# Thirty-two experts of a two-block kernel: a fifth pair of weight buffers, four of them rotating, and the first item's rows gathered ahead

## What is computed

```python
# t: the 256 tokens after norm and modulation; w_g, w_u: 32 x 1024 x 256, w_d: 32 x 256 x 1024
p_group = softmax(tf @ w_rg + b_rg)              # one of 4 groups
pv, pi  = top_k(softmax(le_g), 2)                # two of the 8 experts of that group
combine = sum(one_hot(ids, 32) * wts[..., None], axis=1)
for e in range(32):
    he  = silu(t @ w_g[e]) * (t @ w_u[e])
    out = out + combine[:, e:e + 1] * (he @ w_d[e])
```

## Time and profile before

| what | value |
|---|---|
| median of the timed runs | 1992.12 us (1991.62 to 1996.06, 3 runs) |
| the profiled execution's own time | 1992.81 us |
| its span, first to last instruction | 1990.9 us |
| PE busy | 1849.2 us, 93% of the span |
| chain that ended last | PE 86%, issue 4%, DVE 4%, DMA 2% |
| DMA | 345.07 MB, mean 173 GB/s over the span |
| PE on L1192, L1177, L1217 in the chain | 5%, 3%, 2% |
| stretch from first pick to the last item's products | about 565 to 843 us |

### The profile page before, as it was taken

The page is one execution under the profiler, slowest core; times in us unless marked ns, Lnnn a source line. Parts: engine busy times, 40 slices in busy tenths (PEclk is TensorE's granted clock), DMA queues, the critical chain, the costliest instruction groups (busy, mean ns, idle before and its releaser), DMA issues.

```text
span 1990.9 us, 33082 instructions
## 1 busy us (share of the span) xinstructions
PE 1849.2 (93%) x12610; PEld 1348.9 (68%) x12610; DVE 1035.5 (52%) x2332; ACT 551.4 (28%) x1185; POOL 54.2 (3%) x76
## 2 busy tenths in 40 slices
PE   6999999999987788899999899999999999999998
PEld 4878788757755566554564688887444465788886
DVE  3366573387442223444778877775987326333311
ACT  3343400172130111221570333332000226244310
POOL 0000000000000000000000011111000000000000
PEclk8999999999998899999999999999999999999999
DMA  9444483423459999630204122223764030144441
GB/s 372 177 190 195 185 359 149 169 86 157 197 241 425 421 418 390 258 127 0 85 2 190 64 84 85 84 84 138 306 252 170 2 108 1 50 155 155 165 187 48
DMA packets 38531, 345.07 MB, mean 173 GB/s; under 512 B 4231, under 2 KB 9102, under 8 KB 10382
## 3 DMA queue, kind: packets, MB, share of 16 engines
q1 hardware_dynamic: 37550, 334.02, 42.7%
q10 hardware_dynamic: 864, 9.44, 1.1%
HBM read 380.14 MB, written 1.05 MB: 191 GB/s over the span
## 4 chain that ended last, share of the span: by engine, by line
PE 86%; issue 4%; DVE 4%; DMA 2%; PEld 2%; ACT 1%; DVEq 0%; SPq 0%; PEldq 0%; ACTq 0%
PE bank L672 49%; PE bank L1428 13%; PE bank L1192 5%; PE bank L1177 3%; PE bank L1217 2%; PE bank L793 2%; PEld bank L672 2%; PE bank L1393 1%; PE bank L1302 1%; PE bank L1310 1%; DMA ring<-in_ada 1%; PE bank L1153 1%; PE bank L1400 1%; PE bank L898 1%; DVE ring L2135 1%
## 5 line engine op out<-in xcount | busy, mean ns | idle before, releaser
L672 PE MATMUL bank<-hn,ring 128*128 128x256 f32 (+2 forms) x2080 | 514.3, 407 | 9.8 <-ACT hn L1526 4.6
L672 PE MATMUL bank<-arena,ring 128*128 128x256 f32 (+2 forms) x1600 | 467.3, 449 | 17.8 <-issue 13.9
L672 PEld LDWEIGHTS bank<-hn,ring 128*128 128x128 f32 (+1 forms) x2080 | 395.3, 191 | 119.2 <-issue 68.6
L672 PEld LDWEIGHTS bank<-arena,ring 128*128 128x128 f32 (+1 forms) x1600 | 298.0, 188 | 180.4 <-issue 148.2
L1428 PE MATMUL bank<-ring 128*128 128x256 f32 x704 | 160.7, 381 | 1.2 <-DVE ring L2762 0.6
L1428 PEld LDWEIGHTS bank<-ring 128*128 128x128 f32 x704 | 133.7, 191 | 21.6 <-issue 2.1
L2022 DVE SCALAR_TENSOR_TENSOR bank<-ring,c_rows 128x1024 f32<-128x1024 f32 x96 | 118.1, 1231 | 21.5 <-DMA ring<-in_ada 16.7
L1428 PE MATMUL bank<-hn,ring 128*128 128x256 f32 x528 | 123.0, 383 | 3.8 <-ACT hn L1882 3.8
L2022 DVE SCALAR_TENSOR_TENSOR ring<-ring,c_rows 128x1024 f32<-128x1024 f32 x96 | 117.2, 1221 | 0.0
L1506 ACT ACTIVATE hn<-resid 128x256 f32<-128x256 f32 (+1 forms) x48 | 22.6, 485 | 336.5 <-DVE resid L2113 336.5
L1428 PEld LDWEIGHTS bank<-hn,ring 128*128 128x128 f32 x528 | 101.4, 192 | 18.5 <-issue 4.6
(11 more groups left out here) (434 smaller groups left out, 2072.5 us busy)
## 6 DMA issues: line engine op xcount, KB each, us to landing
ring<-in_ada SPq DMA_DIRECT2D x28, 2048.0 KB, 8.2
ring<-in_up SPq DMA_DIRECT2D x44, 1024.0 KB, 4.8
ring<-in_egu SPq DMA_DIRECT2D x20, 2048.0 KB, 16.3
ring<-in_edn SPq DMA_DIRECT2D x32, 1024.0 KB, 14.2
hn<-in_egu ACTq DMA_DIRECT2D x15, 2048.0 KB
arena<-in_egu SPq DMA_DIRECT2D x11, 2048.0 KB, 13.9
ring<-in_down SPq DMA_DIRECT2D x16, 1408.0 KB, 9.3
ring<-in_adat SPq DMA_DIRECT2D x8, 2048.0 KB, 11.8
```

What stands on the lines that cost most here:

```text
L672: last = mm(out, lhs(i), rhs(i), start=i == 0, stop=i == k - 1)
```

## The change

- A fifth pair of buffers. `gu_more` is a new gate_up buffer in `arena`, which grows by 3328 columns (13 KB per partition); the new down buffer is the upper half of the ring's slot 5. The space comes from the scratch that is set aside for descriptors: `dynamic_dma_scratch_size` goes from its default of 16384 bytes per partition to 1024. A sum buffer of the norm (`sq_acc`) moves to the end of `arena`.
- Items 0 to 4 take a pair each, item e from 5 on takes pair `(e - 5) % 4`, over items take pair 4, whose gate_up buffer is the one over `hn`.
- The order becomes 0 to 4, 5, 6 o0, 7 8 o1, 9 10 o2, 11 12 o3, and so on, with two over items after 20, 24 and 28 and none after 30.
- SP loads gate_up 0, down 0, gate_up 1, gate_up 2, down 1 to 4 and gate_up 3 ahead of `iota`, gate_up 4 into `hn` after it.
- PE waits for both halves of `pick`, gathers the 32 rows of item 0 into bank 6 (16 small matmuls), then block k = 0 of the gather of all, then `step(0)`, then blocks 1 to 7. ACT copies the first rows to `x_t[0]` and does item 0's Silu between blocks 2 and 3.
- Four semaphores that nothing used are gone.

```diff
+OVER_BUFFER = 4
+
+
 def item_order():
 
-    first, pairs = 4, (NE - 4) // 2
-    order, over = list(range(first)), NE
-    for pair in range(pairs):
-        order += [first + 2 * pair, first + 2 * pair + 1]
-        for _ in range(pair < pairs - 1) if pair not in (4, 9) else range(2):
+    order, over = list(range(OVER_BUFFER + 1)), NE
+    for item in range(OVER_BUFFER + 1, NE):
+        order.append(item)
+        for _ in range(0 if item % 2 or item > NE - 4 else 2 if item in (20, 24, 28) else 1):
             order.append(over)
             over += 1
     assert over == ITEMS and len(order) == ITEMS
@@ -65,7 +67,7 @@
 
 
 ORDER = item_order()
-BUFFER = [item if item < 4 else 3 if item >= NE else (item - 4) % 3 for item in ORDER]
+BUFFER = [item if item < 5 else OVER_BUFFER if item >= NE else (item - 5) % OVER_BUFFER for item in ORDER]
 USE = [BUFFER[:i + 1].count(b) for i, b in enumerate(BUFFER)]
 BEFORE = [max((j for j in range(i) if BUFFER[j] == b), default=None) for i, b in enumerate(BUFFER)]
 AT = {item: i for i, item in enumerate(ORDER)}
...
 SLOTW = 4096
+MORE = 3328
...
-        arena = sb("arena", [P, 12288])
+        arena = sb("arena", [P, 12288 + MORE])
...
+            if q == 0:
+                return ring[:, 6 * SLOTW - SLOTW // 2:]
+            q -= 1
             return ring[:, 2 * SLOTW + q * SLOTW // 2:2 * SLOTW + (q + 1) * SLOTW // 2]
...
-        sq_acc = out_tmp.rearrange("p a t -> p (a t)")
+        sq_acc = arena[:, 12288 + MORE - 2 * T:]
...
+        gu_more = arena[:, 12288 + MORE - 2 * T - SLOTW:12288 + MORE - 2 * T]
...
-            return (gu_arena, slot(1), slot(0), hn[:, :, :].rearrange("p k t -> p (k t)"))[q]
+            return (gu_more, gu_arena, slot(1), slot(0), hn[:, :, :].rearrange("p k t -> p (k t)"))[q]
...
             sp.wait_ge(phase, 3 * (MOE_PHASE - 2))
             load_gate_up(0)
+            load_down(0)
+            load_gate_up(1)
             sp.wait_ge(slot_free[1], used[1] + 1)
-            load_gate_up(1)
+            load_gate_up(2)
             sp.wait_ge(slot_free[2], used[2] + 1)
-            for i in range(2):
-                load_down(i)
+            for e in (1, 2):
+                load_down(e)
             sp.wait_ge(slot_free[3], used[3] + 1)
-            for i in range(2, 4):
-                load_down(i)
+            for e in (3, 4):
+                load_down(e)
             sp.wait_ge(slot_free[0], used[0] + 1)
-            load_gate_up(2)
+            load_gate_up(3)
             sp.wait_ge(phase, 3 * (MOE_PHASE - 1))
             sp.dma_start(iota, dr["iota"]).then_inc(s["moe_iota"], 16)
             sp.wait_ge(s["tok_mm"], 1)
-            load_gate_up(3)
-
-            for e in range(4, NE + 1):
+            load_gate_up(4)
+
+            for e in range(5, NE + 1):
                 if e < NE:
                     sp.wait_ge(s["moe_h"], BEFORE[AT[e]] + 1)
                     load_gate_up(e)
-                if e >= 5:
+                if e >= 6:
                     sp.wait_ge(s["moe_y"], BEFORE[AT[e - 1]] + 1)
                     load_down(e - 1)
...
-                    if i >= 1:
+                    if i == 0:
+                        pe.wait_ge(s["moe_Xev"], 1)
+                    else:
                         pe.wait_ge(s["moe_xt"], i)
...
-                            last = mm(bank[x][CAP * q:CAP * q + CAP, 0:P], x_t[x][:, k, :] if i else xs[:, k, 0:CAP],
+                            last = mm(bank[x][CAP * q:CAP * q + CAP, 0:P], x_t[x][:, k, :],
...
-            step(0)
+            pe.wait_ge(s["tok_ev"], 1)
+            pe.wait_ge(s["moe_G"], TT)
+            for k in range(KD):
+                for t in range(TT):
+                    last = mm(bank[6][:, k * CAP:(k + 1) * CAP], h_tok[:, t, k * P:(k + 1) * P], pick[:, t, 0:CAP],
+                              start=t == 0, stop=t == TT - 1)
+            last.then_inc(s["moe_X"], 1)
+            for k in range(KD):
+                if k >= 4:
+                    pe.wait_ge(s["moe_Xev"], k - 2)
+                if k == 1:
+                    step(0)
+                for t in range(TT):
+                    last = mm(bank[2 + k % 4][:, :], h_tok[:, t, k * P:(k + 1) * P], pick[:, t, :], start=t == 0, stop=t == TT - 1)
+                last.then_inc(s["moe_X"], 1)
+                if k == 4:
+                    pe.wait_ge(s["route_dve"], 4)
+                    mm(bank[7][0:NE, NE + 2:NE + 3], C("trix", NE)[:, 0:NE], cnt[0:NE, 1:2], start=True, stop=True) \
+                        .then_inc(s["route_pe"], 1)
+
...
             pe.wait_ge(s["route_dve"], 5)
             token_rows()
+            pe.wait_ge(s["moe_Xev"], KD + 1)
             mm(bank[5][:, 0:4 * OVER], ones[0:NE, :], table[0:NE, :], start=True, stop=True).then_inc(s["route_pe"], 1)
...
+            act_e.wait_ge(s["moe_X"], 1)
+            fn(x_t[0], bank[6][:, 0:KD * CAP].rearrange("p (k x) -> p k x", k=KD), ACT.Copy).then_inc(s["moe_Xev"], 1)
             for k in range(KD):
                 if k == 1:
                     act_e.wait_ge(s["route_dve"], 3)
                     fn(g4b, g4a, ACT.Exp)
                     fn(t2d, t2d, ACT.Exp).then_inc(s["route_act"], 1)
-                act_e.wait_ge(s["moe_X"], k + 1)
+                if k == 3:
+                    act_e.wait_ge(s["moe_h"], 1)
+                    fn(hsil[:, 0, :], bank[0][:, 0:64], ACT.Silu).then_inc(s["moe_silu"], 1)
+                act_e.wait_ge(s["moe_X"], k + 2)
                 fn(xs[:, k, 0:NPOS], bank[2 + k % 4][:, :], ACT.Copy).then_inc(s["moe_Xev"], 1)
...
+                    if i > 0:
+                        fn(hsil[:, i % 2, :], bank[i % 2][:, 0:64], ACT.Silu).then_inc(s["moe_silu"], 1)
...
-                        over_load(next_over[i], w_gate_up(3), "egu", gu_landed[3])
+                        over_load(next_over[i], w_gate_up(OVER_BUFFER), "egu", gu_landed[OVER_BUFFER])
...
-                        over_load(next_over[v], w_down(3), "edn", dn_landed[3])
+                        over_load(next_over[v], w_down(OVER_BUFFER), "edn", dn_landed[OVER_BUFFER])
...
-            pool.wait_ge(s["moe_Xev"], KD)
+            pool.wait_ge(s["moe_Xev"], KD + 1)
...
-    nc = bacc.Bacc("TRN2", target_bir_lowering=False, num_devices=1)
+    nc = bacc.Bacc("TRN2", target_bir_lowering=False, num_devices=1, dynamic_dma_scratch_size=1024)
```

More of the change, by code:

```diff
@@ L286, in build @@
         gqa_landed = [sem(f"gqa{i}_landed") for i in range(KVG)]
-        gu_landed = [sem(f"gate_up{i}_landed") for i in range(4)]
-        dn_landed = [sem(f"down{i}_landed") for i in range(4)]
+        gu_landed = [sem(f"gate_up{i}_landed") for i in range(OVER_BUFFER + 1)]
+        dn_landed = [sem(f"down{i}_landed") for i in range(OVER_BUFFER + 1)]
         phase = sem("phase_ended")
         names = """
-            vec_turned vec_ready csil_zeroed csil_ready rows_ready ada_mm ada_rows ada_cols ada_ready
+            vec_turned csil_zeroed csil_ready rows_ready ada_mm ada_rows ada_cols ada_ready
             sq_ready ss_ready std_ready hn_scaled hn_ready rope_reduced rope_sin
-            dt_pe dt_dve dt_act group_done gsm_ready
+            dt_pe dt_dve dt_act gsm_ready
             ssm_z ssm_zs ssm_x ssm_acc ssm_taps ssm_skip ssm_conv ssm_tok ssm_bcb ssm_xw ssm_E ssm_Ex ssm_from ssm_state ssm_stT ssm_seg
-            ssm_exp ssm_M ssm_yd ssm_yoff ssm_yo ssm_y ssm_sq ssm_ss ssm_std ssm_normed
+            ssm_exp ssm_M ssm_yd ssm_yoff ssm_y ssm_sq ssm_ss ssm_std ssm_normed
             out_mm out_sig out_ev gemm_mm gemm_ev
@@ L1144, in _ @@
             mm(bank[7][0:NE, NE + 1:NE + 2], sel_both, ones[:, 0:1], start=True, stop=True).then_inc(s["route_pe"], 1)
-            pe.wait_ge(s["tok_ev"], 1)
-            for k in range(KD):
-                if k >= 4:
-                    pe.wait_ge(s["moe_Xev"], k - 3)
-                for t in range(TT):
-                    if k == 0:
-                        pe.wait_ge(s["moe_G"], t + 1)
-                    last = mm(bank[2 + k % 4][:, :], h_tok[:, t, k * P:(k + 1) * P], pick[:, t, :], start=t == 0, stop=t == TT - 1)
-                last.then_inc(s["moe_X"], 1)
-                if k == 4:
-                    pe.wait_ge(s["route_dve"], 4)
-                    mm(bank[7][0:NE, NE + 2:NE + 3], C("trix", NE)[:, 0:NE], cnt[0:NE, 1:2], start=True, stop=True) \
-                        .then_inc(s["route_pe"], 1)
-            pe.wait_ge(s["moe_Xev"], KD)
-            def token_rows():
-                for b, pair in ((6, (pos_a, pos_b)), (7, (t2b, t2c))):
-                    for x, value in enumerate(pair):
-                        for t in range(TT):
-                            last = mm(bank[b][:, x * T + t * P:x * T + (t + 1) * P], value[:, t, 0:1].to_broadcast([P, P]), ident,
-                                      start=True, stop=True)
-                last.then_inc(s["moe_rows"], 1)
             def combine(v):
@@ L1219, in step, with token_rows @@
                     last.then_inc(s["moe_y"], 1)
-            step(0)
```

(13 more changed lines are left out.)

11 lines of the change are left out of this document (6 added, 5 removed).

## The result

| | before | after |
|---|---|---|
| median of 5 runs each | 1996.06 us (1991.62 to 1996.96) | 2005.96 us (2002.77 to 2007.68) |
| ratio of the runs | 1 | 1.0046, 95% interval 1.0033 to 1.0059 |
| span of the profiled execution | 1990.9 us | 2004.2 us |

The change costs 9.2 us (6.6 to 11.8). I had forecast 1.4 us, which can't be told from no change, and a range up to 2001.0: the measured change is well clear of no change, and 2005.96 lies outside the range. Part of the miss in absolute time is the base: before's three runs had a median of 1992.12, five have 1996.06. The rest is the forecast.

What follows compares the result with a forecast made beforehand. It took weight delivery by DMA to bound places 1 to 17 and PE pauses, inferred as late instructions, places 20 to 46. +2.9 at place 20 and -1.5 after gave +1.4 us: 1993.5 us, range 1984 to 2001.

Steps and rivals of the forecast that it cites:

- `iota`: SP's queue ahead of the gather: one pair more lands `iota` at 569.6, `pick` 4.8 us later, PE begins at 572.6.
- Rival 1: SP's queue: `iota` lands beside the other loads, `pick` is not late, everything to place 1 4.8 us earlier; 1988.7, chance 0.07.
- The gather of the first rows: PE ahead of place 1: small gather 6.6 us with 5 us at half clock; place 1 at 597.6, +9.7.
- rival 3: Gather: instruction pauses in blocks 1 to 7, perhaps half clock throughout the small gather and block 0; slower, 2000.5, chance 0.31.
- The buffer freed early: After early `step(0)`: gate_up buffer free about 2.8 us earlier than 585.73, at 582.9; DMA idle again until place 1 is multiplied.
- To the last place: Places 1 to 20: weights still decide, place 20 at 698.9 against 695.96, so +2.9 from +9.7 at place 1.
- line of delivery: Places behind the three pairs loaded over items: DMA's delivered weights set PE's pace, coming 1.6 us later for the same item.
- rival 2: Places 1 to 20: 16.1 us of weight waits and their half clock fall away, place 20 about 690; 1984.5, chance 0.23.
- Places 20 to 46: Last 26 places: fourth rotating pair fills DMA holes, transfers end some 10 us earlier; -1.5 us, between -4 and +3.
- the four numbers: Predicted whole times: forecast 1993.5, rival 1 1988.7, rival 2 1984.5, rival 3 2000.5 us.

Runs made afterwards that it cites:

- e1: After without the gather of the first rows: fifth pair, its item order and its loads, with before's gather and step(0); ratio to before 0.9998, -0.4 us.
- e5: Before with `iota` late, by a dummy pair of loads (3.1 MB, read by nobody) ahead of it on SP's queue; ratio to before 1.0022, +4.4 us.
- e4: After plus eight matmuls with unread results while PE waits for `pick`, to keep the clock up; ratio to before 1.0029, +5.8 us.
- e2: Before with only the gather of the first rows and step(0) moved ahead, four pairs and old order kept; ratio to before 1.0035, +7.0 us.
- e3: After with `iota` in a buffer of its own, loaded some 70 us earlier; ratio to before 1.0017, +3.4 us.
- e9: Before with SP's weight loads from item 4 on cut to a sixteenth of their columns, result not the kernel's; ratio to before 0.9677, -64.5 us.
- e8: e6 plus eight and four small filling matmuls ahead of and behind the routing matmuls; ratio to before 0.9992, -1.6 us.
- e11: e6 with double over items after items 12, 14, 16 instead of 20, 24, 28, plus the filling matmuls of e8; ratio to before 0.9983, -3.4 us.
- e6: e1 with `iota` in a buffer of its own, loaded early as in e3; ratio to before 0.9986, -2.8 us.

## Why the prediction was wrong

- **`iota`: right.** 13.3 us to landing, forecast 13.4; PE's gather began at 572.86, forecast 572.6. By the Trainium skill's rule that the semaphore's increment waits for all earlier writes of its DMA engine (DMA: Bandwidth & Descriptors, Queues, rings and completion order) the whole backlog is paid; after, e1 and e5 (13.3, 13.4, 13.3) agree; in e4 it was 14.8. Rival 1 is out.
- **The gather of the first rows: right in kind, too small.** I let PE's work run at the lower clock for 5 us; it did for 12, from 572.86 to about 585. The small gather took 7.00 (forecast 6.6), block 0 3.76 (1.8), `step(0)` 2.83 (1.96); place 1 started at 600.89, forecast 597.6. The 3.3 us are these three terms. e4 shows them going with the clock. I had this as the second half of rival 3.
- **The buffer freed early: right in mechanism, late in time.** Issues at 586.27 and 602.9 (forecast 582 to 583, 599), so the first is no earlier than in before (585.73), DMA idle in two pieces, 24.0 us from 560 to 604 by the windows.
- **"To the last place": this step failed.** It let the weights' line of delivery set place 20, so that 9.7 us at place 1 became 2.9 at place 20. The measured shift is 13.0 at place 1, 10.75 at place 20 (706.71 against 695.96) and 10.9 at the end. The step said that at place 20 "weights still decide". They did not: gate_up 15 landed at 701.94, and PE came 4.8 us behind it. (The line was late as well: I had put this landing at 696.9.) Of the 9.5 us by which the last group missed the forecast (841.94 against 832.4), 3.3 are place 1, 4.5 this step (105.8 us for 101.3) and 1.7 the next one. e2, e3, e4 and e5, each of which moves place 1 by something else, move the last group by 8.3, 5.1, 6.6 and 4.0 us against before for 8.1, 5.9, 8.6 and 3.5 at place 1.
- **What the step left out: a pause can stand in for a wait.** I took the later of two arrivals at place 20, the line's and PE's own at 5.19 us a place (98.6 us for 19 places). In after the 19 places took 105.8 us, with 5.5 us of waits for over items and 19.0 us of pauses one after the other; in before they took 108.0, with 16.1 us of waits and 7.5 of pauses. 10.6 us of waits went and 11.5 us of pauses came. The 2.2 us that were gained are busy time (80.7 us for 83.0), with less of it at the lower clock (granted clock 0.95 for 0.91). Counting PE's matmul records in steps of 126 shows it one by one: each kernel passes 14 such steps in these places, and q8 moves 14 packets. In after a pause stands at 12 of them; in before at 6, and each run of missing ones follows a wait. While PE waits for weights, the next packets come in. Below is PE's idle time from place 1 to 20 by line, before and then after (columns: line, what, records, busy us and mean ns, idle us before it by releaser).

```profile
L1177 PE MATMUL bank<-ring,arena 32*128 32x256 f32 x272 | 21.9, 424 | 1.1 <-issue 1.1
L1217 PE MATMUL bank<-ring 128*32 128x256 f32 x288 | 19.8, 385 | 1.8 <-issue 1.8
L1192 PE MATMUL bank<-ring,arena 128*32 128x128 f32 x515 | 18.3, 292 | 10.0 <-issue 9.5 <-DVE ring L2595 0.4
L1192 PE MATMUL bank<-hn,arena 128*32 128x128 f32 x448 | 17.1, 311 | 6.4 <-issue 6.4
L1192 PE MATMUL bank<-arena 128*32 128x128 f32 x256 | 8.5, 285 | 5.0 <-issue 5.0
```

```profile
L1205 PE MATMUL bank<-ring 128*32 128x256 f32 x288 | 21.1, 399 | 5.7 <-issue 5.7
L1163 PE MATMUL bank<-ring,arena 32*128 32x256 f32 x272 | 20.0, 401 | 3.2 <-issue 3.2
L1180 PE MATMUL bank<-arena 128*32 128x128 f32 x448 | 15.4, 274 | 5.7 <-issue 5.7
L1180 PE MATMUL bank<-hn,arena 128*32 128x128 f32 x384 | 15.2, 315 | 8.4 <-issue 8.4
L1180 PE MATMUL bank<-ring,arena 128*32 128x128 f32 x384 | 11.6, 273 | 0.4 <-DVE ring L2618 0.4
L1188 PE MATMUL bank<-consts,ring 128*32 128x64 f32 x152 | 7.5, 222 | 1.7 <-issue 1.6 <-DVE ring L2624 0.2
```

  "issue" sums to 23.8 us in before and 24.6 in after. Ahead of and inside the gate and up groups it falls from 20.9 to 14.1; in the down products, the combine and the transposes, where all of it lies at the steps of 126 and so is pauses, it rises from 2.9 to 10.5. The waits had covered pauses that now stand alone, and that is why rival 2, which let 16 us of waits fall away, did not come about.
- **Places 20 to 46: no gain.** 135.2 us against 135.06; I had put -1.5, inside my bounds of -4 and +3. The prediction's 4.24 us for a place without pauses was too long: e9 has 3.94, and so has before between places 18 and 19 (688.09 to 692.03).
- **Rival 3** named a slower kernel for a wrong place: blocks 1 to 7 took 7.14 us for 16 records and 5.42 for 12, as before, with no pause among them. Its half clock was there, and its 2000.5 was the nearest of the four numbers; it came near in part for a reason that did not occur.

By the runs, of 9.2 us the gather ahead is +7.0, the late `iota` +4.4, and the fifth pair -2.8 to -4.8: a sum of 6.6 to 8.6, inside the interval of 6.6 to 11.8. Taken out of after instead of put into before, the gather ahead is worth 9.6 us (after against e1) and the late `iota` 5.8 (after against e3), each within some 3 us. What stays open: why e8 and e11 gain nothing from an earlier place 1 beyond the wait at place 18, and what makes the instruction packets late, which no run here isolated.

## What to carry to other kernels

A small transfer that an engine is waiting for must not stand behind a backlog on its queue: each MB ahead of it cost 2.3 us here, and 256 KB of SBUF kept for it bought that back (e3, e6). Before a wait is counted as a gain, ask what stall lies under it: take the pace of a stretch that has none of these waits, and if the stretch with them is no slower by their sum, they are cover and not cost. Work that is moved ahead of a bound stage delays that whole stage by its price at the clock it will really get, which here, after waits of PE of 3 and 8 us, was the lower one.

## What the runs showed of the hardware

- A matmul with 128x128 weights and 32 columns in float32 costs 0.114 us a record at the full clock (3.65 us for 32, e4), nearly as much as with 128 columns (0.128), and 0.219 at half (7.00, after and e2).
- After a pause of 3 us (e2, e3) as after 8 (after) all 32 small records ran at 1.2 GHz, and block 0 of the gather behind them too, wholly in e2 and after (3.76 us) and nearly so in e3 (3.63, against 1.97 in e4).
- From place 20 on a place of 104 matmul records took 3.94 us beside light DMA traffic (e9) and 5.19 beside full traffic (before), where no gate_up load of SP's queue was waited for: the same instructions took a third longer.
- Each pause of PE ended 1.2 to 1.6 us after a 16 KB packet of the instruction queue had ended (25 pauses in before, 30 in after). A wait of PE for data let the packets run ahead, and the next pauses were missing.
